# Last combine step and twelve convolution taps as diagonal products in a two-layer decoder trunk

## What is computed

```python
def causal_dwconv(z, hist, w):                      # w: (31, 512) for the long convolution
    zp = jnp.concatenate([hist, z], axis=1)
    y = lax.conv_general_dilated(zp, w[:, None, :], window_strides=(1,), padding='VALID', ...
                                 feature_group_count=c)
    return y, zp[:, -(k - 1):]

# mixer_cd of layer 1
glu = h[..., :D_C] * jax.nn.sigmoid(h[..., D_C:2 * D_C])
cc, new_hist_c = causal_dwconv(glu, hist_c, conv_c_w)
c_out = jax.nn.silu(layer_norm(cc + conv_c_b, ln_c_g, ln_c_b))
...
y = jnp.einsum('nte,ed->ntd', jnp.concatenate([c_out, d_out], axis=-1), w_out)

# end of each layer: h = LN(alpha*h + HierMoE(h)); each row goes through two experts
hid = jax.nn.silu(hg) * hu * gates.astype(x.dtype)[..., None]
y = jnp.einsum('mef,efd->md', hid, w_down)
```

## Time and profile before

| | us |
|---|---|
| runs of the program | 1661.15, 1661.51, 1665.81; median 1661.51 |
| the profiled execution | 1660.55 |
| its span | 1658.8 |

### The profile page before, as it was taken

How to read it: one execution, slowest core, us unless ns; L and a number is a source line. 1 busy time by engine, 2 the same in 40 slices (tenths; PEclk the granted TensorE clock), 3 DMA queues, 4 the chain that set the end, 5 groups by cost and what they waited for, 6 DMA issues and landing times.

```text
span 1658.8 us, 21602 instructions
## 1 busy us (share of the span) xinstructions
PE 1434.2 (86%) x8337; PEld 1174.5 (71%) x8337; DVE 1107.8 (67%) x1361; ACT 702.6 (42%) x632; POOL 261.1 (16%) x331
## 2 busy tenths in 40 slices
PE   7999999899599999997999958998995899999950
PEld 5786788767477777774489946887674778777730
DVE  3526661447598888884469995714565988888926
ACT  3423022322477667771131213314323777767711
POOL 1110110002012111213100002200021112222216
PEclk9999999999799999999989988999997999999985
DMA  8610164333589999997653001742425899999963
GB/s 326 240 54 1 59 229 177 140 115 130 199 320 350 344 347 345 364 351 259 186 166 102 26 1 40 255 179 86 169 102 196 311 346 348 341 340 358 353 238 111
DMA packets 107121, 356.72 MB, mean 215 GB/s; under 512 B 12521, under 2 KB 42249, under 8 KB 90129
## 3 DMA queue, kind: packets, MB, share of 16 engines
q1 hardware_dynamic: 86784, 308.43, 51.4%
q0 software_dynamic: 16704, 43.44, 7.2%
q10 hardware_dynamic: 3553, 3.73, 0.7%
HBM read 343.33 MB, written 28.72 MB: 224 GB/s over the span
## 4 chain that ended last, share of the span: by engine, by line
PE 40%; DVE 25%; DMA 17%; issue 8%; ACT 6%; POOL 2%; ACTq 0%; DVEq 0%; SPq 0%; POOLq 0%
PE ps L671 15%; DMA raw<-in_w_gate_dram 12%; DVE wlo L1977 9%; PE ps L700 7%; ACT whi L1542 3%; PE ps L1240 3%; DVE xlo L1748 3%; PE ps L719 2%; PE ps L1116 2%; DVE wlo L1745 2%; PE ps L925 2%; DVE arena L2272 2%; PE ps L972 2%; PE ps L950 2%; DVE gb L2272 2%
## 5 line engine op out<-in xcount | busy, mean ns | idle before, releaser
L1977 DVE TENSOR_TENSOR wlo<-raw,whi 128x2048 fp32r<-128x2048 f32 x192 | 435.6, 2285 | 88.6 <-ACT whi L1542 88.4
L1542 ACT ACTIVATE whi<-raw 128x2048 fp32r<-128x2048 f32 x192 | 366.8, 1916 | 158.1 <-DMA raw<-in_w_down_dram 105.7
L1116 PE MATMUL ps<-whi,xhi 128*128 128x512 f32 x768 | 291.7, 407 | 37.3 <-issue 17.5
L1116 PE MATMUL ps<-wlo,xhi 128*128 128x512 f32 x768 | 285.2, 398 | 0.0
L1116 PE MATMUL ps<-whi,xlo 128*128 128x512 f32 x768 | 284.8, 398 | 0.0
L1116 PEld LDWEIGHTS ps<-whi,xhi 128*128 128x128 f32 x768 | 144.0, 191 | 75.5 <-issue 45.6
L1116 PEld LDWEIGHTS ps<-wlo,xhi 128*128 128x128 f32 x768 | 146.6, 191 | 34.8
L1116 PEld LDWEIGHTS ps<-whi,xlo 128*128 128x128 f32 x768 | 146.7, 191 | 32.8
L1748 DVE TENSOR_TENSOR xlo<-ps,xhi 128x1024 fp32r<-128x1024 f32 (+2 forms) x108 | 107.2, 994 | 72.1 <-ACT xhi L1371 34.5
L1745 DVE TENSOR_TENSOR wlo<-raw,whi 128x2048 fp32r<-128x2048 f32 x48 | 108.5, 2285 | 64.9 <-ACT whi L1366 64.9
L671 PE MATMUL ps<-whi,xhi 128*128 128x512 f32 (+1 forms) x400 | 130.0, 407 | 10.1 <-DVE wlo L1745 6.2
(11 more groups left out here) (337 smaller groups left out, 2071.6 us busy)
## 6 DMA issues: line engine op xcount, KB each, us to landing
raw<-in_w_gate_dram SPq DMA_DIRECT2D x66, 1024.0 KB, 8.7
raw<-in_w_up_dram SPq DMA_DIRECT2D x66, 1024.0 KB, 7.5
raw<-in_w_down_dram SPq DMA_DIRECT2D x64, 1024.0 KB, 7.4
raw<-in_w_k_dram SPq DMA_DIRECT2D x8, 1024.0 KB, 7.5
raw<-in_w_v_dram SPq DMA_DIRECT2D x8, 1024.0 KB, 10.0
raw<-in_w_q_dram SPq DMA_DIRECT2D x8, 1024.0 KB, 8.7
whi_rows<-in_cache_mem_k_dram SPq DMA_DIRECT2D x8, 1024.0 KB, 5.1
raw<-in_w_o_dram SPq DMA_DIRECT2D x8, 1024.0 KB, 5.5
```

Source lines behind the costliest of these rows:

```text
L1116: mm = pe.matmul(ps[:, bank + half, :], x[:, k, :], w[s][:, at:at + 512], start=(k == 0 and n == 0), stop=(k == 2 * k_unit - 1 and n == 2))
L1542: act.activation(whi[s % RING][:, :], raw[r % RING][:, :], ACT.Copy).then_inc(sig("hi_made"), 1)
L1977: dve.tensor_tensor(wlo[s % RING][:, :], raw[r % RING][:, :], whi[s % RING][:, :].bitcast(F32), ALU.subtract).then_inc(sig("lo_made"), 1)
```

## The change

Convolution: of group 3, the last 12 taps (19 to 30) leave VectorE. ScalarE makes a 128x128 matrix for each with the tap's weights on the diagonal (`tap_diag`, in the part of `xhi` that is free then), three of them ahead of the copy for `d_hi`, nine behind it. TensorE multiplies them by the shifted `gluT` and sums in bank 2, behind the transposes of the tails and ahead of the first short half. VectorE adds the bank after its own sum. Since bank 2 is taken, the short half of tile 1 is moved: it comes behind the first three `conv_rows`.

Last combine: SyncE fetches both rows of every tile with one DMA for each tile, the sample tile first, into `raw[t]`, which the experts no longer need, once GpSimd has seen the stores land (`rows_ready`). For tiles 0 to 3 TensorE sums in PSUM: `h` by the identity, and the two rows by diagonals of `rw` that ScalarE makes. VectorE takes statistics and gain from PSUM, and does the bias for every tile itself; the sample tile's sums stay on VectorE. GpSimd keeps the deviation and the stores.

```diff
@@ allocation @@
+        xhi_first = nc.alloc_sbuf_tensor_at("xhi_first", [P, G4 * TOK], F32, offset=xhi_at)
+        LAST_ORDER = (LASTT,) + tuple(range(LASTT))
+        choice_diag = area(8448, 2 * LASTT * P, "p (t j n) -> p t j n", t=LASTT, j=2)
+        sample_back = area(6400, 2 * D, "p (j n) -> p j n", p=NS, j=2)
+        PE_TAPS = range(TAPS_C - 12, TAPS_C)
+        TAPS_BANK = 2
+        tap_diag = [xhi_first[:, n * P:(n + 1) * P] for n in range(len(PE_TAPS))]
@@ SyncE @@
+                else:
+                    sp.wait_ge(sig("rows_ready"), past("rows_ready") + 1)
+                    by_row = y_dram.rearrange("(j r) n -> r j n", j=2)
+                    for t in LAST_ORDER:
+                        if t == LASTT:
+                            sp.dma_start(sample_back, by_row[SEQ:TOK]).then_inc(sig("samples_back"), 16)
+                        else:
+                            sp.dma_start(raw[t][:, :].rearrange("p (j n) -> p j n", j=2), by_row[t * P:(t + 1) * P]).then_inc(sig(f"raw_landed{t}"), 16)
@@ TensorE, combine_columns @@
+                if l == DEPTH - 1:
+                    pe.wait_ge(sig(f"scaled{l}"), past(f"scaled{l}") + TILES)
+                    for t in range(LASTT):
+                        for half in halves:
+                            pe.matmul(pair_flat(t)[:, half], ident[:, :], h[:, t, half], start=True, stop=False)
+                    for t in range(LASTT):
+                        wait_rows_back(pe, t)
+                        pe.wait_ge(sig("choice_diag"), 2 * (t + 1))
+                        for j in range(2):
+                            for half in halves:
+                                mm = pe.matmul(pair_flat(t)[:, half], choice_diag[:, t, j, :],
+                                               raw[t][:, j * D + half.start:j * D + half.stop], start=False, stop=(j == 1))
+                        mm.then_inc(sig("rows_summed"), 1)
@@ TensorE, conv_layer @@
+                for n, tap in enumerate(PE_TAPS):
+                    pe.wait_ge(sig("tap_diag"), past("tap_diag") + n + 1)
+                    mm = pe.matmul(ps[:, TAPS_BANK, 0:SEQ], tap_diag[n], gluT[:, G4 - 1, tap:tap + SEQ],
+                                   start=(n == 0), stop=(n == len(PE_TAPS) - 1))
+                mm.then_inc(sig("taps_mm"), 1)
                 pe.wait_ge(sig("d_hi"), 1)
                 pe.wait_ge(sig("d_lo"), 1)
-                for t in range(2):
-                    row_product("out1", t, rows(t), cols(t), t, "wout1", t == 0, False, SHORT_FIRST[:2])
+                short_half(0)
...
                 for t in range(3):
                     conv_rows(t)
+                short_half(1)
                 conv_columns(0)
                 conv_rows(3)
                 conv_columns(1)
@@ ScalarE @@
-                act.activation(xhi[:, G4:KC, :], cd, ACT.Copy).then_inc(sig("d_hi"), 1)
+                for n, tap in enumerate(PE_TAPS):
+                    act.activation(tap_diag[n], ident[:, :], ACT.Copy, scale=ccol[:, G4 - 1, tap:tap + 1]).then_inc(sig("tap_diag"), 1)
+                    if n == 2:
+                        act.activation(xhi[:, G4:KC, :], cd, ACT.Copy).then_inc(sig("d_hi"), 1)
...
                     for t in range(LASTT):
-                        act.activation(h[:, t, :], h[:, t, :], ACT.Copy, scale=rstd[:, t:t + 1]).then_inc(sig("last_scaled"), 1)
+                        for j in range(2):
+                            act.activation(choice_diag[:, t, j, :], ident[:, :], ACT.Copy, scale=rw[:, t, j:j + 1]).then_inc(sig("choice_diag"), 1)
@@ VectorE @@
+            def last_combine(l):
+                for n in range(TILES + 1):
+                    if n < TILES:
+                        t = LAST_ORDER[n]
+                        if t == LASTT:
+                            wait_rows_back(dve, t)
+                            link(dve.scalar_tensor_tensor(hv, sample_back[:, 0, :], rw[0:m, t, 0:1], hv, ALU.mult, ALU.add))
+                            link(dve.scalar_tensor_tensor(hv, sample_back[:, 1, :], rw[0:m, t, 1:2], hv, ALU.mult, ALU.add))
+                        else:
+                            dve.wait_ge(sig("rows_summed"), past("rows_summed") + t + 1)
+                            summed = pair_flat(t)
+                        statistics(tag, n, m, [summed[:, 0:512], summed[:, 512:1024]])
+                    if n:
+                        add_bias(tag, n - 1, before_m, h[0:before_m, before_t, :], gb[0:before_m, 1, :])
+                    if n < TILES:
+                        normalise(tag, n, m, hv, summed, gb[0:m, 0, :], tag)
@@ VectorE, taps @@
-                TAPS = [(g, k) for g in range(G4) for k in range(TAPS_C)]
+                TAPS = [(g, k) for g in range(G4) for k in range(TAPS_C) if g < G4 - 1 or k not in PE_TAPS]
+                        if (g, k) == TAPS[-1]:
+                            dve.wait_ge(sig("dve_chain"), max(written.values()))
+                            link(dve.tensor_tensor(acc[:, g, 0:SEQ], acc[:, g, 0:SEQ], odd_taps[g % 2], ALU.add))
+                            dve.wait_ge(sig("taps_mm"), past("taps_mm") + 1)
+                            dve.tensor_tensor(acc[:, g, 0:SEQ], acc[:, g, 0:SEQ], ps[:, TAPS_BANK, 0:SEQ], ALU.add).then_inc(sig("conv"), 1)
@@ GpSimd, combine of the last layer @@
+                    pool.tensor_tensor(wait_mark[:, 0:1], minus_half[0:1, :], minus_half[0:1, :], ALU.add).then_inc(sig("rows_ready"), 1)
+                    for n in range(TILES + 1):
+                        if n < TILES:
+                            reciprocal_deviation(tag, n, rows(LAST_ORDER[n]))
+                        if n:
+                            pool.wait_ge(sig("last_row"), n)
+                            pool.dma_start(out, h[0:rows(t), t, :]).then_inc(sig("stored"), 16)
```

More of the change, by code:

```diff
@@ L256, in trunk_kernel @@
     share("early_b", [("x_landed", 32), ("cache_b", EARLY_LANDED["b"])])
+    share("tails_tr", [("tails_tr", 4), ("rows_summed", LASTT)])
+    share("flat_ready", [("flat_ready", 2), ("rows_ready", 1)])
+    share("early_b", [("x_landed", 32), ("cache_b", EARLY_LANDED["b"]), ("samples_back", 16)])
+    share("hist1_tr", [("hist1_tr", 1), ("taps_mm", 1)])
+    share("glu_gate", [("glu_gate", 4), ("tap_diag", 12)])
     share("norm_res", [(f"{stage}_res", TILES) for stage in ("out0", "o0", "out1", "o1")])
@@ L283, in trunk_kernel @@
         h = sb("h", [P, TILES, D])
+        xhi_at = nc.sbuf_base
         xhi = sb("xhi", [P, KC, TOK], F32R)
+        xhi_first = nc.alloc_sbuf_tensor_at("xhi_first", [P, G4 * TOK], F32, offset=xhi_at)
         xlo = sb("xlo", [P, KC, TOK], F32R)
@@ L2229, in combine @@
                         normalise(tag, t - 1, m, hv, hv, gb[0:m, 0, :], tag)
-                        if tag != LAST_NORM or t == TILES:
-                            add_bias(tag, t - 1, m, hv, gb[0:m, 1, :])
-                if lo_keys:
-                    for t in range(3):
-                        columns_lo(tag, t, rows(t))
-                    for key in lo_keys:
-                        make_lo(key)
-                    for t in range(3, TILES):
-                        columns_lo(tag, t, rows(t))
+                        add_bias(tag, t - 1, m, hv, gb[0:m, 1, :])
+                for t in range(3):
+                    columns_lo(tag, t, rows(t))
+                for key in lo_keys:
+                    make_lo(key)
+                for t in range(3, TILES):
+                    columns_lo(tag, t, rows(t))
             def conv_layer():
@@ L2385, in _ @@
                 further(l)
-                combine(l, [("wglu", g) for g in range(G4)] if l < DEPTH - 1 else [])
+                if l < DEPTH - 1:
+                    combine(l, [("wglu", g) for g in range(G4)])
+                else:
+                    last_combine(l)
         @block.gpsimd
```

41 lines of the change are left out of this document (22 added, 19 removed).

## The result

The changed kernel takes 1642.17 us, the median of 4 runs (1636.17 to 1645.65), against 1661.33 us for the kernel before in the same comparison (4 runs, 1655.57 to 1665.81). The ratio is 0.9874, with a 95% interval of 0.9839 to 0.9909. The forecast was 1645.0, in a range of 1638.5 to 1652.0.

The account below looks back on a forecast made before the run. The prediction took VectorE's taps to bound the convolution and no engine for long to bound the last stage. From 1660.55 us it took 3.0 (convolution) and 13.4 (tail), 1644.1, given as 1645 against the median; range 1638.5 to 1652.

Parts of the forecast that it names:

- VectorE's gain: Convolution: twelve taps fewer save 8.0 us, less 0.8 for an addition and 0.9 for diagonals, leaving 6.3 us.
- Such a product has a row: Convolution: each fp32 tap product on TensorE priced at 0.43 us, from a row of 15 in 6.60 us.
- rival E: Convolution: fp32 tap products take 0.86 us, TensorE hardly idles and keeps the upper clock level; 1643.2 us, chance 2%.
- TensorE's tap products ended by 979: Convolution: sign that the forecast is right, the twelve tap products finished by 979 in the new trace.
- The moved half: Convolution: 24 matmuls, some 6.1 us, ahead of tile 0's columns; 6.3 us of VectorE turn into 3.0.
- Rival A: Convolution: the moved half costs the whole gain, leaving the tail's alone; 1648 us, chance 14%.
- C: Convolution: the moved half is hidden because tile 0's columns would otherwise wait for ScalarE; 1641.7 us, chance 11%.
- The tail: Last combine: one early fetch, sums on TensorE, VectorE the bound at 4.05 us per tile; gain 13.4 us.
- The 2.3 us of latency in the sum: Last combine: latency taken off a 4.9 us landing of 1 MB, to give 2.6 us per MB.
- B: Last combine: the tail is bound by the fetch, 5 us per MB instead of 2.6; 1649 us, chance 8%.
- rival D: Last combine: fetches follow one another at 10.0 us each, making the kernel slower; 1667.6 us, chance 1%.
- The sum: Whole kernel: 1660.55 - 3.0 - 13.4 = 1644.1 us, given as 1645 against the median of the runs.

Follow-up runs that it names:

- e4_six_products: Changed kernel with the last six of twelve tap products left out and TensorE waiting for all twelve diagonals first; convolution stage 40.7 us against 38.1.
- e11_eight_taps: Changed kernel with eight taps on TensorE instead of twelve, four given back to VectorE; convolution stage 42.1 us against 38.1, one execution 1635.11 us.
- e3_moved_half: Kernel before with only the second short half moved behind the first three row transposes; convolution stage 47.2 us against 42.8 to 44.2, one execution 1675.68 us.
- e8_quarters: Changed kernel with half of the moved half put behind the rows of tile 3; convolution stage 36.1 us against 38.1, one execution 1638.51 us.
- e5_no_identity: Changed kernel without the eight identity products that bring h into PSUM; tail 43.0 us against 39.6.
- e2_tail_only: Kernel before with only the last combine's part of the change; ratio 0.9934 to the kernel before, tail 38.8 us, convolution stage 44.2 us.
- e6_fetch_only: Kernel before with only the last layer's rows fetched by SyncE into raw all at once; ratio 0.9983 to the kernel before, tail 50.0 us against 54.4.

## Why the prediction was right, and where it was not

**VectorE's gain, 6.3 us forecast, 6.4 measured.** The sixteen taps, the delay by the diagonals (0.9 forecast; the first tap starts 0.85 us later than before, 0.76 of it the wait in the row) and their 0.3 each came out.

**The step that failed** is "Such a product has a row: 15 in 6.60 us ... so 0.43 apart". The row counts instructions, and a float32 product is two of them. The order of the changed kernel lists L1346 twelve times; its trace has it 24 times. The source view of L1240 of the kernel before, and of L1346 of the changed one (count; ns of an instruction, three values from the shortest to the longest; from when to when; form):

```profile
L1240 PE MATMUL ps<-raw,arena x128: 592/592/697, 767.4 to 823.8; 128*128 128x512 f32 x128
```

```profile
L1346 PE MATMUL ps<-arena,xhi_first x24: 590/592/785, 975.1 to 985.2; 128*128 128x512 f32 x24
```

A product therefore takes 2 x 0.43 = 0.86 us at the 2.4 GHz level. This is rival E, to which I gave 2%. I had read a count of records as a count of products. The sign "TensorE's tap products ended by 979", 11.2 us behind the stage's start, failed with it: they ended 13.6 us behind. That the program's time still came out within 3 us of the forecast is luck in part, since the wrong price left the stage short of its gain by only 1.7 us and did the tail no harm.

The Trainium skill, page FP8 and Floating Point Precision, section TensorE Precision Notes, states four passes through the array for true FP32. Four passes of 512 columns at 2.4 GHz are 0.85 us, an estimate from that page; this trace agrees, with 0.86.

**What followed from it.** The taps ended near 985 and the first half at 991.3, TensorE idled for 2.2 us and not 6, and the transposes took 1.5 us at the upper level and not 2.8. The columns of tile 0 came 28.8 us behind the stage's start (forecast 30.8) and its product 32.4 (34.2). The gain is 4.7, where the forecast had 3.0 and E 4.8. The idle time ahead of the transposes is what parts the runs: they were at the upper level behind 2.20 to 2.62 us of it, in all profiles with twelve taps on TensorE, and at the lower one behind 3.51 (`e4_six_products`), 8.45 (`e11_eight_taps`) and 12.27 (before). In `e4_six_products` the work ahead of the idle time was shorter and in part at the lower level, too, and no run parts the one from the other.

**The moved half** did what the forecast said: it stands on the path, without a wait, and takes part of the gain. `e3_moved_half` prices it at 3.0 to 4.4 us with the clock at the lower level ahead of it; in the changed kernel it is 5.4 us of work on the path (995.0 to 1000.4). The columns of tile 0 still come 3.4 us earlier than before (28.8 us behind the stage's start for 32.2), since the row transposes start 6.4 us earlier and are 1.3 shorter. The other 1.3 of the 4.7 are behind the columns, where TensorE is now at the upper level throughout and SiLU no longer waits for the table load. Rival A (the whole gain lost) and C (nothing lost) are both out: `e8_quarters` gets 2 us of it back by another order.

**The tail, 13.4 forecast, 14.8 measured.** SyncE's first issue came 4.25 us behind the tail's start (forecast 4.27). TensorE started on tile 0 10.3 us behind the tail's start (forecast 9.5), VectorE on the samples 8.1 (7.0), so the rows landed a little later than forecast. The 2.3 us of latency in the sum stand in no row; the samples took 3.4 us to land, not 2.7, and from 1608.60 to 1611.80 the DMAs moved 387 GB/s, 2.7 us per MB, near the 2.6 assumed. DMA issues of the changed kernel from 1600 us on (KB each, median us to landing):

```profile
raw<-expert_rows SPq DMA_DIRECT2D x4, 1024.0 KB, 9.7
arena<-expert_rows SPq DMA_DIRECT2D x1, 256.0 KB, 3.4
```

Rivals B and D are out, since TensorE waited for no row after tile 0. Four products per tile took 3.4 us, the number forecast, by two errors that cancel: twice the instructions, at twice the clock. The clock stayed up because the identity products took 7.1 us, not 3.4, and left 2.26 us of idle time, not 6; without them it fell (`e5_no_identity`). VectorE's period was 3.80 us, not 4.05; it waited for no deviation at the end, since the last one was ready 1.9 us behind the end of its statistics, and not 2.9: GpSimd's second operation for it took 0.57 us beside a VectorE operation that reads PSUM, where the row of before has 1.59 beside one that reads two operands from SBUF. The last store was issued 30.9 us behind the start (forecast 31.4), and the span ended 8.7 us behind it (9.3 before, 9.6 in the forecast), so 0.9 of the 1.4 us beyond the forecast lie behind the last issue. From tile 3's statistics to the last issue the prediction has 6.1 us in its sum, 6.5 where it prices a fetch at 5 us per MB and 5.2 in rival D; the trace has 5.5.

**The sum.** 4.7 + 14.8 = 19.5 us; the medians differ by 19.2, and the forecast by 16.5. In the later comparison the ratio of the same kernel, 0.9835, is 24 to 31 us. In its profile the stages give 4.8 and 14.9; 3.2 us more are in the part between them and 1.2 ahead of both. The table above puts most of the variation into the experts of layer 1; what makes it there, and whether the change has a hand in it, I did not settle.

## What to carry to other kernels

Count a product's instructions before pricing it by a row: a row's count is one of records. Work moved onto TensorE can be worth more than the time that it frees elsewhere, where it shortens TensorE's idle stretch ahead of a burst on the path, and less where it doesn't: of the twelve taps eight took 5.3 us from VectorE and gained 0.7 to 2.1, and four more took 2.7 and gained 4.0. When the effect looked for is smaller than the kernel's own scatter, measure the stage between two marks, and don't claim the total for it.

## What the runs showed of the hardware

The granted clock stayed at 1.00 over idle times of 2.20 us (changed kernel) and 2.62 us (`e8_quarters`), and fell within idle times of 3.51 us (`e4_six_products`) and 8.45 us (`e11_eight_taps`). The time of its return differed between executions of the same code: the four us from 7.9 us behind the start of the row transposes on had a clock of 0.79 in the kernel before and 0.50 in `e2_tail_only`.

A VectorE operation on 1024 columns with both operands in SBUF (L1790 of `e6_fetch_only`) took 1.24 us with no GpSimd addition beside it, and 2.35 beside one of 2.33.
